# Expert stage of a two-block transformer kernel: the list of experts ahead of the token tables, and two weight remainders on GpSimd

## The reference

```python
counts = jnp.bincount(e_flat, length=N_EXPERTS_2)
padded = (counts + MOE_BLOCK - 1) // MOE_BLOCK * MOE_BLOCK
...
blk_expert = jnp.clip(jnp.searchsorted(p_ends, jnp.arange(n_blk) * MOE_BLOCK, side='right'), 0, N_EXPERTS_2 - 1)
...
hb = jax.nn.silu(xb @ w_gate[e]) * (xb @ w_up[e])
return hb @ w_down[e]
```

## Time and profile before

| | |
|---|---|
| time, median of 3 runs | 2977.89 us (2973.08 to 2992.28) |
| span of the profiled execution | 2993.4 us |
| TensorE busy | 2706.4 us (90%) |
| VectorE busy | 1462.5 us (49%) |
| ScalarE busy | 1095.7 us (37%) |
| GpSimd busy | 852.0 us (28%) |
| products of the up matrices (L1783) | 561.5 us busy |
| low parts of the up matrices (L2011, DVE) | 265.6 us busy, 2291 ns each |
| gathers of rows (L1691) | 58, median 10.1 us to landing |

### The profile page before, as it was taken

The page is one execution under the profiler, slowest core; times in us unless marked ns, Lnnn a source line. Parts: engine busy times, 40 slices in busy tenths (PEclk is TensorE's granted clock), DMA queues, the critical chain, the costliest instruction groups (busy, mean ns, idle before and its releaser), DMA issues. The chain is left out here.

```text
span 2993.4 us, 33502 instructions
## 1 busy us (share of the span) xinstructions
PE 2706.4 (90%) x12036; PEld 1994.2 (67%) x12036; DVE 1462.5 (49%) x1816; ACT 1095.7 (37%) x1437; POOL 852.0 (28%) x686
## 2 busy tenths in 40 slices
PE   4999899999999799948999799999999989798887
PEld 3899466777768677736655365557777868676665
DVE  4196342212223577753266544433532543677776
ACT  3011442000012377751133344441332232377775
POOL 1242422212212134512100223323333322134444
PEclk9999899999999699968999899999999999799999
DMA  3110212112114499952522323322111123499996
GB/s 94 30 50 21 42 33 62 49 35 56 35 57 148 164 350 347 346 164 69 210 57 53 91 58 86 85 72 81 42 42 49 49 82 129 186 335 320 321 313 203
DMA packets 212869, 375.65 MB, mean 125 GB/s; under 512 B 40760, under 2 KB 159880, under 8 KB 189992
## 3 DMA queue, kind: packets, MB, share of 16 engines
q1 hardware_dynamic: 195280, 340.77, 34.2%
q0 software_dynamic: 17280, 33.60, 4.6%
q10 hardware_dynamic: 216, 0.07, 0.0%
HBM read 326.80 MB, written 72.48 MB: 133 GB/s over the span
## 5 line engine op out<-in xcount | busy, mean ns | idle before, releaser
L2011 DVE TENSOR_TENSOR moe_run_w_low_up<-moe_run_w,moe_run_w_high_up 128x2048 fp32r<-128x2048 f32 x116 | 265.6, 2291 | 137.3 <-ACT moe_run_w_high_up L1846 137.3
L1846 ACT CAST moe_run_w_high_up<-moe_run_w 128x2048 fp32r<-128x2048 f32 x116 | 221.2, 1907 | 148.2 <-DMA moe_run_w<-w_gate 65.0
L1783 PE MATMUL moe_run_up<-moe_run_w_high_up,moe_run_xT_high 128*128 128x512 f32 x464 | 193.5, 417 | 33.9 <-issue 33.6
L1783 PE MATMUL moe_run_up<-moe_run_w_low_up,moe_run_xT_high 128*128 128x512 f32 x464 | 184.1, 397 | 0.0
L1783 PE MATMUL moe_run_up<-moe_run_w_high_up,moe_run_xT_low 128*128 128x512 f32 x464 | 183.9, 396 | 0.0
L1338 DVE TENSOR_TENSOR merge_gated<-merge_branch,merge_gate 128x512 f32<-128x512 f32 x48 | 33.2, 692 | 280.3 <-ACT merge_gate L1322 280.1
L1201 ACT ACTIVATE mla_probs<-mla_scores 128x512 f32<-128x512 f32 x192 | 94.2, 491 | 177.1 <-PE mla_scores L1133 92.6
L1322 ACT ACTIVATE merge_gate<-merge_gates 128x512 f32<-128x512 f32 x48 | 28.7, 598 | 346.9 <-PE merge_branch L122 346.9
L1146 PE MATMUL mla_out<-mla_probs,mla_v 128*65 128x512 f32 (+3 forms) x384 | 150.4, 487 | 0.0
L1691 POOL DMA_INDIRECT moe_run_x<-v,moe_run_rows x58 | 129.7, 2236 | 50.0 <-POOL moe_run_rows L1727 37.9
L1783 PEld LDWEIGHTS moe_run_up<-moe_run_w_high_up,moe_run_xT_high 128*128 128x128 f32 x464 | 88.4, 190 | 69.3 <-issue 52.5
(11 more groups left out here) (538 smaller groups left out, 7256.5 us busy)
## 6 DMA issues: line engine op xcount, KB each, us to landing
moe_run_w<-exp_w SPq DMA_DIRECT2D x72, 1024.0 KB, 9.4
moe_run_w<-w_gate SPq DMA_DIRECT2D x34, 1024.0 KB, 9.9
moe_run_w<-w_up SPq DMA_DIRECT2D x34, 1024.0 KB, 13.6
moe_run_w<-w_down SPq DMA_DIRECT2D x34, 1024.0 KB, 7.9
out_h<-x SPq DMA_DIRECT2D x16, 512.0 KB, 4.5
v<-out_v SPq DMA_DIRECT2D x16, 512.0 KB, 2.8
mla_raw_q_then_weights<-w_in SPq DMA_DIRECT2D x16, 512.0 KB, 3.9
rnn_raw<-w_in SPq DMA_DIRECT2D x16, 512.0 KB
```

The source lines that it names most:

```text
L1783: last = pe.matmul(up[p][:], a, w, start=(h == 0 and k == 0), stop=(h == 1 and k == 3 * HK - 1))
L1846: act.copy(hi[p][j], raw[p][j][:]).then_inc(s_hi[j], 1)
L2011: dve.tensor_tensor(lo[p][j], raw[p][j][:], hi[p][j].bitcast(F32), ALU.subtract).then_inc(s_lo[j], 1)
```

## The change

Three edits, all in `run_experts`, so that they work in both expert stages. First, VectorE computes the list of experts (`half`, `last2`, `passes`, `along`, `sb_at`, `below`, `sb_e`) as soon as the running sum `ends` is there, instead of behind the one-hot tables, and copies the list out ahead of the reduction of `at`; TensorE turns the list's column before the products for the token ids instead of behind them. Second, GpSimd makes the low parts of block 0's two up matrices, behind its constants and ahead of its wait for the token table. Third, VectorE's first low parts are put in another order: the down matrix of block 0 first, then one up matrix of block 1 ahead of each block's rows.

```diff
                 for p in range(2):
                     own(pool.memset(x[p][:], 0.0))
+                for j in range(2):
+                    pool.wait_ge(s_hi[j], 1)
+                    pool.tensor_tensor(lo[0][j], raw[0][j][:], hi[0][j].bitcast(F32),
+                                       ALU.subtract).then_inc(s_lo[j], 1)
...
                 own(TS(by_e[:, :, 0:1], nb[:][:, :, None], float(P), None, ALU.mult))
+                blocks = ends[:, E - 1:E]
+                own(TS(half[:], blocks, 0.5, 0.25, ALU.mult, ALU.add))
+                TS(last2[:], blocks, 2.0, -1.0, ALU.mult, ALU.add)
+                own(TS(half[:], half[:], ROUND, ROUND, ALU.add, ALU.subtract))
+                TS(passes[:], half[0:1, :], 1.0, None, ALU.subtract)
...
+                TS(sb_e[:], sb_e[:], E - 1.0, None, ALU.min).then_inc(s_bcol, 1)
...
-                dve.wait_ge(s_brow, 1)
-                own(dve.tensor_copy(expert[:], ps_row[0:1, 0:NB]))
-                dve.sem_inc(s_list, 1)
...
+                dve.wait_ge(s_brow, 1)
+                dve.tensor_copy(expert[:], ps_row[0:1, 0:NB]).then_inc(s_list, 1)
                 own(dve.tensor_reduce(at[:], t3, AX.X, ALU.add))
...
-                rest(0, 0, 0)
-                rest(0, 0, 1)
+                rest(0, 0, 2)
+                dve.wait_ge(s_lo[0], 1)
+                rest(0, 1, 0)
                 rest_of_rows(0, 0)
                 dve.wait_ge(s_wsum, 2)
                 dve.tensor_copy(place_w[:], ps_w[:, 0:NB]).then_inc(s_weights, 1)
-                rest(0, 1, 0)
+                dve.wait_ge(s_lo[1], 1)
+                rest(0, 1, 1)
                 rest_of_rows(0, 1)
-                rest(0, 1, 1)
-                rest(0, 0, 2)
                 gated(0, 0, True)
```

More of the change, by code:

```diff
@@ L1750, in _ @@
                 pe.matmul(ps_rank, strict[:], flat, start=True, stop=True).then_inc(s_rank, 1)
+                pe.wait_ge(s_bcol, 1)
+                pe.matmul(ps_row[0:1, 0:NB], sb_e[0:NB, :], cst["ident"][0:NB, 0:NB], start=True,
+                          stop=True).then_inc(s_brow, 1)
                 for k in range(2):
@@ L1756, in _ @@
                 last.then_inc(s_ids, 1)
-                pe.wait_ge(s_bcol, 1)
-                pe.matmul(ps_row[0:1, 0:NB], sb_e[0:NB, :], cst["ident"][0:NB, 0:NB], start=True,
-                          stop=True).then_inc(s_brow, 1)
                 def turn_rows(i, p, first=False):
@@ L1957, in _ @@
                 own(TS(by_e[:, :, 0:1], nb[:][:, :, None], float(P), None, ALU.mult))
+                blocks = ends[:, E - 1:E]
[3 more added lines that the diff above has]
+                TS(passes[:], half[0:1, :], 1.0, None, ALU.subtract)
+                own(TS(along[:], odd[:], -1.0, 0.5, ALU.mult, ALU.add))
+                own(TT(along[:], along[:], s_id[:], ALU.mult))
+                own(STT(out=along[:], in0=odd[:], scalar=-0.5, in1=along[:], op0=ALU.mult, op1=ALU.add))
+                own(STT(out=sb_at[:], in0=odd[:], scalar=blocks, in1=along[:], op0=ALU.mult, op1=ALU.add))
+                own(TS(below[:], ends[:], sb_at[:], None, ALU.is_le))
+                own(dve.tensor_reduce(sb_e[:], below[:], AX.X, ALU.add))
+                TS(sb_e[:], sb_e[:], E - 1.0, None, ALU.min).then_inc(s_bcol, 1)
                 place_e = t3[:, 1].rearrange("p t e -> p (t e)")
@@ L1964, in _ @@
                 own(TT(t3, oh, place[:, None, :, :].broadcast_to((P, 2, NT, E)), ALU.mult))
-                blocks = ends[:, E - 1:E]
-                TS(half[:], blocks, 0.5, 0.25, ALU.mult, ALU.add)
-                TS(last2[:], blocks, 2.0, -1.0, ALU.mult, ALU.add)
+                dve.wait_ge(s_brow, 1)
+                dve.tensor_copy(expert[:], ps_row[0:1, 0:NB]).then_inc(s_list, 1)
                 own(dve.tensor_reduce(at[:], t3, AX.X, ALU.add))
-                own(TS(half[:], half[:], ROUND, ROUND, ALU.add, ALU.subtract))
                 own(TS(blk[:], at[:], 1.0 / P, -(P - 1.0) / (2 * P), ALU.mult, ALU.add))
@@ L1980, in _ @@
                     dve.sem_inc(s_hot, 1)
[L1982 to L1988, removed]
                 dve.wait_ge(s_exp, 2)
@@ L1995, in _ @@
                 own(TT(weights[:, 1, :], weights[:, 0, :], ex[:], ALU.mult))
-                TS(passes[:], half[0:1, :], 1.0, None, ALU.subtract)
                 own(dve.memset(token[:, NB:], S))
```

## The result

The changed kernel takes 3005.61 us (median of 4 runs, 3003.22 to 3007.06) against 2980.99 us before. The ratio is 1.0066, 95% interval 1.0049 to 1.0083, or 19.7 us on 2981: the change makes the kernel slower, by less than 1%. The profiled executions have spans of 3003.4 us after and 2993.4 before; the one before lies above the median of its kernel, so spans are not compared.

The account below looks back on a forecast made before the run. The prediction took loads to bound the steady loop and the routing to set its start; 2 x 0.85 for the list plus 8.5 and 9.1 for GpSimd, loads 0, gave 19.3 us on 2977.89: 2997 us, range 2978 to 3006.

Parts of the forecast that it names:

- What bounds the kernel: Both expert stages: the steady loop is held by its loads; the routing's end on VectorE sets when the loop starts.
- The loads gain nothing: Block 2's early loads: 0 us, since SyncE stands at block 3's down matrix; otherwise up to 16 us a stage.
- rival 2: Expert loop: the early loads pay through a backlog at block 3's down matrix; 2965 us, without the lock 2948; chance 0.04.
- rival 3: Gathers meet early loads, or the clock rises later: 2.5 to 5 us more a stage, 3002 to 3007 us; chance 0.07.
- The list: Routing: computing the list of experts ahead of the tables costs net +0.85 us a stage.
- The lock: Routing: GpSimd's subtractions hold the shared SBUF port for whole instructions, delaying VectorE by 8.5 and 9.1 us.
- The sum: Both stages: list 2 x 0.85 plus GpSimd's low parts 8.5 and 9.1 gives 19.3 us, so 2997 us.
- Rivals 1 and 4: Routing: first, GpSimd's subtractions yield or share, 2980 us, chance 0.11; fourth, lock lasts for pieces, 2988 us, chance 0.08.

Follow-up runs that it names:

- v_queue_after: The changed kernel with a block's down matrix asked for behind the next block's two up matrices; ratio 1.0071 to the kernel before.
- e_held: The changed kernel with SyncE held before block 2's loads until the low part of block 0's down matrix is made; ratio 1.0059 to the kernel before.
- e_pool: The kernel before with GpSimd's two subtractions and the new order of low parts, the list in its old place; ratio 1.0094.
- the list alone: The changed kernel with GpSimd's two subtractions back on VectorE, the list staying early; ratio 1.0008 to the kernel before.
- e_one: The changed kernel with one of GpSimd's two subtractions back on VectorE, first behind the routing; ratio 1.0035 to the kernel before.
- e_pieces: The changed kernel with each GpSimd subtraction cut into 8 of 256 elements a partition; ratio 1.0041 to the kernel before.

## Why the prediction was right, point by point

- **What bounds the kernel.** That the end of the routing moves the whole stage was right: the sum of the table agrees with the times. "The loop is held by its loads" was too narrow. Without the waits for loads (v_queue_after) it is not shorter, and the chain that ends last in the second stage is TensorE's in the kernel before and that of the accumulating stores in the changed one.
- **The loads gain nothing.** Right in the result (e_held), which also refutes rival 2, and SyncE did stand at block 3's down matrix. The reason was only half of it: the prediction gave up to 16 us a stage as the price of that stand, and v_queue_after, in which the queue doesn't stand there, has the same time. Where the gain of the first 60 us goes is open: other waits stand in its place, and the granted clock is lower.
- **A cost of the loads that the sum did not have:** their meeting with the gathers. In rival 3 it was at 2.5 to 5 us a stage. The changed kernel shows 0.6 us in the first stage; e_pool shows 4.5 and 4.3.
- **The list.** +0.85 us forecast, 0.75 and 0.77 measured.
- **The lock.** The mechanism was as told, the size somewhat smaller: GpSimd's subtraction took 4.5 us, not 4.7, and the chain moved by 7.3 us (8.5 forecast) and 8.2 us (9.1 forecast), token table of the changed kernel less that of the list alone. In the first stage the two instructions last 4.3 and 3.7 us longer than before, and of this the 0.65 us that VectorE waited before for TensorE's totals passed during the first hold. The second hold is the shorter one because the PSUM copy and the reductions, which are not held, ran beside GpSimd's second subtraction ahead of it. The term left out both; it had the copy itself late by 8.5 us, and it came 3.6 us late.
- **The sum.** 19.3 us forecast, 19.7 by the ratio, of which 17.8 are seen in front of the first products. The agreement is in part luck: the lock was 2.1 us too large in it, and about as much lies outside the routings, where one profile can't place it. The median of 3005.6 is 8.6 us above the 2997 forecast, of which 3 are the base (2980.99 with a fourth run). It lies outside the likeliest case, 2992 to 3002, and inside the range only by 0.4 us.
- **Rivals 1 and 4.** No lock: refuted by e_pool and e_one. A lock for pieces: refuted by the 4.49 us instruction; the hold was for a whole GpSimd instruction at the lengths tried (4.5 us, 1.8 us, and about so at 0.7 us).

## What to carry to other kernels

An idle engine is free only if its instructions don't take what the busy one needs: count GpSimd work that reads SBUF, beside a VectorE chain on the critical path, at nearly its whole duration (7.3 and 8.2 us of 9.0 here), and look at which VectorE instructions have two SBUF inputs or run from SBUF with a constant. Ahead of moving a transfer earlier, ask what is behind it on the same engines: here full DMA engines turned an early load into a later gather, and a load that was free to go in the wrong microsecond cost 4.5 us. Where a chain is late by its own filling work while another engine computes for it, take filling work out of that place, not put it in front.

## What the runs showed of the hardware that was not expected

- A VectorE instruction of 8 elements a partition can last 4.49 us; the busy time of VectorE (1469.2 us after) counts such waits as work, so a profile by busy time alone shows nothing wrong.
- GpSimd's float32 subtraction of 2048 elements takes 4.5 us, 2.0 times VectorE's 2.29. A memset of 2048 elements on GpSimd takes 1.8 us.
- With 16 short GpSimd instructions in a row (0.72 us each), VectorE's instructions that are held follow each other at 0.68 us, about one per piece (e_pieces). Instructions with one input of a single element a partition are not held there: 0.13 to 0.15 us.
